# Inverse root of the head outputs: a power on GpSimd and a DRAM row in place of a product with a diagonal

## The chip, the cores and the metric

The program runs on one core of a Trainium2 chip. Its measure is the device time of one execution in microseconds (us), median over the runs. Below, PE is TensorE, DVE is VectorE, ACT is ScalarE, POOL is GpSimd and SP is SyncE; "PEld" is TensorE's weight load, and a "q" behind an engine's name is its instruction queue.

## The reference, cut to what matters

The model has two layers over 512 tokens of width 1024. Layer 0 is a differential attention with 8 heads, followed by a convolutional gated MLP and a gated embedding. Only the attention's last step, the norm of each head's output over its 128 columns, is touched:

```python
def rmsnorm(x, g):
    xf = x.astype(jnp.float32)
    inv = lax.rsqrt(jnp.mean(xf * xf, axis=-1, keepdims=True) + RMS_EPS)
    return (xf * inv).astype(x.dtype) * g

def diff_attention(...):
    ...
    o = lax.map(one_block, (q_blocks, jnp.arange(n_blocks)))
    o = o.transpose(1, 0, 3, 2, 4).reshape(B, S, N_HEADS, V_DIM)
    o = rmsnorm(o, sub_g) * (1.0 - lambda_init)
    return o.reshape(B, S, N_HEADS * V_DIM) @ w_o
```

All matrix products are made exact to float32 by splitting each operand into a high and a low part (three products of high and low for each one of the reference).

## The kernel before, in words

Weights come in 190 units of 512 KB into four raw slots (`w_raw`); SP issues a load as soon as DVE has made the low part of the unit that held the slot (`lo_done`). ACT makes the high part (`split_hi`, L383), DVE the low part (`split_lo`, L804), and PE uses them. The activations stand transposed: features on the 128 partitions, the 512 tokens along the free dimension.

The order of every engine is written out by hand in the program, one block for each engine, and semaphores join them. The attention runs in a loop over heads, `for hd in range(N_HEADS)`, that each engine has a copy of. For head hd, PE does:

- the key projection (24 products of 512 columns into bank 1), then half of the query projection into bank 0, the ten transposes of the weights of head hd-1 (`head_transposes`, L1347), the rest of the query projection;
- `output_spread(hd - 2)`: two products of 512 columns, a matrix of ones with a diagonal matrix, into bank 6 (L1263, L1264);
- `head_product(hd - 1)`: softmax weights by values, into bank 1 (L1238 to L1240 with wT and v);
- the scores of head hd (L1334), and `output_sums(hd - 1)`: sums of squares over the partitions, one column for each token tile (L1258).

DVE copies the keys out (`k_rows`, L902), then for head hd-2 makes the inverse of the root (`output_inverse`: L965, and the helper `spread` with L818, L820 and L822, which writes the diagonal `diag`), the low parts of keys, transposed weights (L954) and queries (L910), the norm of head hd-2 (`output_norm`, L971) with its low part (L976), then the maxima of the scores (`softmax_first`, L926, and L915, which ACT's exponentials wait for), the variance of head hd-1 (`output_variance`, L960) and the second half of the softmax (L936 to L943). ACT does the root of head hd-2 (`output_rms`, L477), the high parts of keys (L447), transposed weights (L456), queries (L451) and of the normed output (L462), the square (L466) and the scaled copy (L473) of head hd-1's output, and the exponentials (L485). The root and the exponential are in different tables, so that a table load stands ahead of each of the two in every head from 2 on.

So the norm of a head goes: variance, root on ACT, inverse and diagonal on DVE, product on PE (which turns the four columns of 128 tokens into a row of 512 that stands in all partitions), product with the output on DVE. It is done one head late. Heads 6 and 7 are normed behind the loop, beside the first products of the output projection (`wo_part`). The copy of a head's output, `o32`, is the buffer `acc`.

Of the kernel before, what the change touches and what calls it, by code (L numbers as in the profile page):

```python
# [8 lines left out]
F32 = mybir.dt.float32  # L9
F32R = mybir.dt.float32r  # L10
BF16 = mybir.dt.bfloat16
ALU = mybir.AluOpType
# [3 lines left out]
P = 128  # L16
# [19 lines left out]
GROUP = SEQ // P  # L36
N_GROUPS = N_HEADS // GROUP
FFN_PARTS = (8, 8, 6)
SLOTS = 4
# [55 lines left out]

def hybrid_trunk(nc, gain_and_x0, xT, pT, weights, final_gain, columns, out):
    with ExitStack() as ctx:
        def sem(name):
            return ctx.enter_context(nc.semaphore(name))

        def sb(name, shape, dt, scope=ctx):
            return scope.enter_context(nc.sbuf_tensor(name, shape, dt))
# [9 lines left out]
        oT_hi = sb("oT_hi", [P, N_HEADS, SEQ], F32R, product)  # L112
        oT_lo = sb("oT_lo", [P, N_HEADS, SEQ], F32R, product)
        product.close()
        product = ExitStack()
# [25 lines left out]
        eps = sb("eps", [P, 1], F32)  # L141
        small = sb("small", [P, 116], F32)
        bs = sb("bs", [P, KT], F32)
# [16 lines left out]
        v_lo = sb("v_lo", [P, TT, N_GROUPS, SEQ], F32R, attn)  # L160
        o32 = acc
        attn.close()
# [50 lines left out]
            sem("pv_done"), sem("o32_done"), sem("osq_done"), sem("oss_done"), sem("ovar_done"), sem("orms_done"),  # L213
            sem("oicol_done"), sem("odiag_done"), sem("ospread_done"))
        onorm_done, ohi_done, olo_done = sem("onorm_done"), sem("ohi_done"), sem("olo_done")

# [55 lines left out]
        orms_col = small[:, 4:8]  # L272
        oicol = small[:, 60:64]
        lam_product = small[:, 64:66]
        oeps = [small[:, 68:72], small[:, 72:76]]
# [5 lines left out]
        final_inv = small[:, 100:104]  # L281
        table_scratch = small[:, 80:81]


# [89 lines left out]
        def _(act):  # L374
# [83 lines left out]
            def output_high(hp):  # L458
                act.wait_ge(onorm_done, hp + 1)
                if hp == 0:  # L460
                    act.wait_ge(pT_done, DEPTH * PLE_KT)
                act.activation(oT_hi[:, hp, :], o32[:, :], ACT.Copy).then_inc(ohi_done, 1)  # L462

# [4 lines left out]
            def output_copy(hp, src):  # L468
                if hp == 0:
                    act.wait_ge(subg_done, 1)  # L470
                else:
                    act.wait_ge(olo_done, hp)
                act.activation(o32[:, :], src[:, :], ACT.Copy, scale=sub_g_scaled).then_inc(o32_done, 1)  # L473
# [283 lines left out]
        def _(pool):  # L757
# [10 lines left out]
                               pattern=[[-1, P]], channel_multiplier=1).then_inc(mask_done, 1)  # L768

            pool.wait_ge(evac_done, result_of("wo", KT - 1))  # L770
            for g, win in enumerate(POOL_WINDOWS):
# [25 lines left out]
        def _(dve):  # L797
# [159 lines left out]
            def output_variance(hp, src):  # L957
                dve.wait_ge(oss_done, hp + 1)
                dve.wait_ge(oeps_done, hp + 1)
                dve.scalar_tensor_tensor(out=ovar, in0=src[:, 0:TT], scalar=float(D_MODEL // P), in1=oeps[hp % 2],  # L960
                                         op0=ALU.mult, op1=ALU.add).then_inc(ovar_done, 1)

            def output_inverse(hp):
                dve.wait_ge(orms_done, hp + 1)
                dve.reciprocal(oicol, orms_col).then_inc(oicol_done, 1)  # L965
                dve.wait_ge(oicol_done, hp + 1)
                spread(oicol, oparts_done, 2 * hp).then_inc(odiag_done, 1)

            def output_norm(hp):
                dve.wait_ge(ospread_done, hp + 1)  # L970
                dve.scalar_tensor_tensor(out=o32[:, :], in0=bank[6][:, :], scalar=float(D_MODEL), in1=o32[:, :],  # L971
                                         op0=ALU.mult, op1=ALU.mult).then_inc(onorm_done, 1)

            def output_low(hp):
                dve.wait_ge(ohi_done, hp + 1)
                dve.tensor_tensor(oT_lo[:, hp, :], o32[:, :], oT_hi[:, hp, :].bitcast(F32), ALU.subtract).then_inc(olo_done, 1)  # L976

# [254 lines left out]
        def _(pe):  # L1232
# [89 lines left out]
            def scores(hd):  # L1322
# [43 lines left out]
            def output_spread(hp):  # L1366
                pe.wait_ge(odiag_done, hp + 1)
                spread(bank[6]).then_inc(ospread_done, 1)
# [30 lines left out]
            for hd in range(1, N_HEADS):  # L1399
# [329 lines left out]
```

## Time and profile before

| what | value |
|---|---|
| time, median of 3 runs | 1112.18 us (1111.61 to 1112.74) |
| span of the profiled execution, first to last instruction | 1110.7 us |
| mean granted TensorE clock, of full speed | 0.995 (1.00 in every stretch between 27 and 260 us) |
| busy: PE, DVE, ACT, POOL | 1093.1, 732.4, 537.4, 19.6 us |
| loop over heads 2 to 7 | about 83 to 188 us of the span |
| one head, from one group of transposes to the next | 17.56 us |
| in 142 to 160 us: PE, DVE, ACT busy | 18.00, 15.63, 14.61 us |

The page gives no time for the profiled execution but its span; the median of the runs is 1.5 us above it.

How to read it. In a timeline the columns are start (us from the span's start), duration (us), engine, source line, operation, output<-inputs, shapes, count; in square brackets stands how long the engine sat idle before, and who ended that. Products are pipelined: a product of 512 columns shows 0.39 us, yet the next starts 0.23 us later, so PE's time is read from starts, not from durations. A list of waits gives who waited for whom, the total in us, how often, and the longest. A group of the page or of the lines gives count | busy us, mean ns of one | idle before. An issue of a transfer gives KB each and the median us from issue to landing.

### The profile page before, as it was taken

The page shows a single profiled execution, that of the slowest core. Times are in us where ns is not written, and L with a number is a line of the kernel's source. Part 1 is how long each engine was busy: PE and PEld are TensorE (multiplying, and loading weights), DVE is VectorE, ACT ScalarE, POOL GpSimd, SP SyncE. Part 2 cuts the span into 40 slices and gives each one's busy share as a digit, 9 for nine tenths or more (in the row PEclk, how much of TensorE's full clock was granted, in tenths as well). Part 3 has the DMA queues.
Part 4 walks back from the last instruction along what each step waited for, and adds up shares of the span by engine and source line. Part 5 has one row for each costly group of instructions (what it writes and reads, how often), then busy time and mean ns, then how long its engine had stood idle before and what let it go on. Part 6 is the DMA issues. An engine that isn't in the chain of part 4 may idle for free.

```text
span 1110.7 us, 14486 instructions
## 1 busy us (share of the span) xinstructions
PE 1093.1 (98%) x5164; PEld 911.0 (82%) x5164; DVE 732.4 (66%) x1136; ACT 537.4 (48%) x799; POOL 19.6 (2%) x62
## 2 busy tenths in 40 slices
PE   9999999999999999999999999999999999999994
PEld 8878888888888888888888888888888888888884
DVE  6568888575775377744776878777437763476836
ACT  6458878454643144421445676544214442244645
POOL 0000000020000000000000000000000000000012
PEclk9999999999999999999999999999999999999997
DMA  8112121222233222332234222232322233222302
GB/s 325 64 58 74 42 76 57 73 101 110 83 107 114 76 95 94 98 116 84 97 98 133 95 76 76 88 102 94 114 76 94 95 103 118 75 101 95 136 36 76
DMA packets 30625, 106.31 MB, mean 96 GB/s; under 512 B 3312, under 2 KB 3312, under 8 KB 30576
## 3 DMA queue, kind: packets, MB, share of 16 engines
q1 hardware_dynamic: 30288, 105.13, 28.1%
q8 instruction: 30, 0.49, 0.2%
q10 hardware_dynamic: 288, 0.53, 0.1%
q14 instruction: 19, 0.16, 0.0%
HBM read 103.55 MB, written 2.10 MB: 95 GB/s over the span
## 4 chain that ended last, share of the span: by engine, by line
PE 92%; DVE 4%; ACT 3%; issue 1%; POOL 0%; DVEq 0%; ACTq 0%; POOLq 0%
PE bank L1238 29%; PE bank L1240 29%; PE bank L1239 29%; PE bank L1334 1%; PE bank L1258 1%; DVE h_tok L1183 1%; ACT probs L485 1%; DVE w_lo L804 1%; DVE c L1189 1%; PE bank L1347 1%; DVE c L1181 0%; PE bank L1299 0%; PE bank L1529 0%; PE bank L1613 0%; PE bank L1526 0%
## 5 line engine op out<-in xcount | busy, mean ns | idle before, releaser
L1238 PE MATMUL bank<-x_hi,w_hi 128*128 128x512 f32 x896 | 350.4, 391 | 0.0
L1240 PE MATMUL bank<-x_hi,w_lo 128*128 128x512 f32 x896 | 348.8, 389 | 0.0
L1239 PE MATMUL bank<-x_lo,w_hi 128*128 128x512 f32 x896 | 348.6, 389 | 0.0
L804 DVE TENSOR_TENSOR w_lo<-w_raw,w_hi 128x1024 fp32r<-128x1024 f32 (+1 forms) x189 | 226.0, 1197 | 52.7 <-ACT w_hi L383 52.6
L383 ACT ACTIVATE w_hi<-w_raw 128x1024 fp32r<-128x1024 f32 (+1 forms) x189 | 193.8, 1031 | 109.8 <-PE bank L1240 109.3
L1240 PEld LDWEIGHTS bank<-x_hi,w_lo 128*128 128x128 f32 x896 | 168.2, 188 | 35.3
L1238 PEld LDWEIGHTS bank<-x_hi,w_hi 128*128 128x128 f32 x896 | 168.2, 188 | 34.7 <-issue 0.4
L1239 PEld LDWEIGHTS bank<-x_lo,w_hi 128*128 128x128 f32 x896 | 168.2, 188 | 34.6
L1238 PE MATMUL bank<-g_hi,w_hi 128*128 128x512 f32 x352 | 136.9, 389 | 0.0
L1239 PE MATMUL bank<-g_lo,w_hi 128*128 128x512 f32 x352 | 136.9, 389 | 0.0
L1240 PE MATMUL bank<-g_hi,w_lo 128*128 128x512 f32 x352 | 136.9, 389 | 0.0
L630 ACT ACTIVATE c<-u,params 128x512 f32<-128x512 f32 x88 | 71.9, 817 | 107.2 <-DVE u L1106 107.2
L1106 DVE TENSOR_TENSOR u<-bank,inv 128x512 f32<-128x512 f32 x88 | 60.6, 689 | 92.6 <-PE bank L1240 92.5
L1012 DVE TENSOR_TENSOR gain_and_h<-bank,gain_and_h 128x512 f32<-128x512 f32 x56 | 38.5, 688 | 97.9 <-PE bank L1240 97.9
L637 ACT ACTIVATE g_hi<-g 128x512 f32 (+1 forms) x44 | 27.8, 632 | 118.8 <-DVE g L1122 118.8
L1239 PEld LDWEIGHTS bank<-g_lo,w_hi 128*128 128x128 f32 x352 | 66.1, 188 | 13.8
L1238 PEld LDWEIGHTS bank<-g_hi,w_hi 128*128 128x128 f32 x352 | 66.1, 188 | 13.7
L1240 PEld LDWEIGHTS bank<-g_hi,w_lo 128*128 128x128 f32 x352 | 66.1, 188 | 13.7
L1116 DVE SCALAR_TENSOR_TENSOR c<-u,params,c 128x512 f32<-128x512 f32 x88 | 66.2, 752 | 9.7 <-DVE c L1111 1.1
L1111 DVE SCALAR_TENSOR_TENSOR c<-u,params,c 128x512 f32<-128x512 f32 x88 | 66.0, 750 | 2.6 <-ACT c L630 1.2
L635 ACT ACTIVATE s<-c 128x512 f32<-128x512 f32 x44 | 27.8, 633 | 74.6 <-DVE c L1116 74.6
L1124 DVE TENSOR_TENSOR g_lo<-g,g_hi 128x512 f32 (+1 forms) x44 | 30.5, 693 | 38.2 <-ACT g_hi L637 38.2
(205 smaller groups left out, 1211.0 us busy)
## 6 DMA issues: line engine op xcount, KB each, us to landing
w_raw<-in_weights SPq DMA_DIRECT2D x189, 512.0 KB, 3.5
gain_and_h<-in_xT SPq DMA_DIRECT2D x7, 256.0 KB, 6.1
out<-emb SPq DMA_DIRECT2D x3, 512.0 KB, 3.1
p_raw<-in_pT SPq DMA_DIRECT2D x1, 1024.0 KB, 10.3
w_raw<-in_weights SPq DMA_DIRECT2D x2, 256.0 KB, 3.6
gain_b<-in_final_gain SPq DMA_DIRECT2D x1, 512.0 KB, 4.2
gain_and_h<-in_gain_and_x ACTq DMA_DIRECT2D x1, 260.0 KB, 3.4
params<-in_columns SPq DMA_DIRECT2D x1, 256.0 KB, 8.1
```

The source lines that it names most:

```text
L383: act.activation(w_hi[s][:, 0:w], w_raw[s][:, 0:w], ACT.Copy).then_inc(hi_done, 1)
L630: act.activation(c32[:, c, :], u32[:, c, PAD:PAD + SEQ], ACT.Identity, scale=tap(layer, 2, j + c * FT), bias=conv_bias(layer, j + c * FT)) ...
L635: act.activation(s32[:, :], c32[:, 0, :], ACT.Silu).then_inc(silu_done, 1)
L804: dve.tensor_tensor(w_lo[s][:, 0:w], w_raw[s][:, 0:w], w_hi[s][:, 0:w].bitcast(F32), ALU.subtract).then_inc(lo_done, 1)
L1012: dve.tensor_tensor(h[:, m, :], src, h[:, m, :], ALU.add).then_inc(evac_done, 1)
L1106: dve.tensor_tensor(u32[:, c, PAD:], bank[2 * v + c][:, :], inv[:, :], ALU.mult).then_inc(evac_done, 1)
L1111: dve.scalar_tensor_tensor(out=c32[:, c, :], in0=u32[:, c, PAD - 1:PAD - 1 + SEQ], scalar=tap(layer, 1, j + c * FT), in1=c32[:, c, :], op0 ...
L1116: dve.scalar_tensor_tensor(out=c32[:, c, :], in0=u32[:, c, PAD - 2:PAD - 2 + SEQ], scalar=tap(layer, 0, j + c * FT), in1=c32[:, c, :], op0 ...
L1124: dve.tensor_tensor(g_lo[:, 2 * a + v, :], g32[:, :], g_hi[:, 2 * a + v, :].bitcast(F32), ALU.subtract).then_inc(glo_done, 1)
L1238: pe.matmul(dst, w1, m1, start=start and i == 0, stop=False)
L1239: pe.matmul(dst, w1, m0, start=False, stop=False)
L1240: last = pe.matmul(dst, w0, m1, start=False, stop=stop and i == len(parts) - 1)
```

## The change

For heads 0 to 5 (`ROW_HEADS` is 6) the way from the variance to the row of inverse roots is another one. POOL raises the variance to the power -0.5 (one operation on 128 x 4 numbers for each head, `tensor_tensor` with `pow` and a constant `minus_half`). ACT, behind its exponentials, issues a transfer of these 512 numbers to a row in DRAM (`row_out`), and in the next head, behind the high part of the keys, waits for it to land and issues a second one that reads the row back into all 128 partitions (`row_in`, into `o_inv`). DVE multiplies by `o_inv` from SBUF in place of bank 6. `output_rms`, `output_inverse` and `output_spread` go for these heads; heads 6 and 7 keep them. The copy `o32` now alternates between two buffers (a new `o32_even` and `acc`), so that `output_copy` waits for the low part of the head before the previous one; and PE no longer waits for `onorm_done` ahead of the last score tile, since bank 6 is not written by a spread in the loop any more.

```diff
+            def row_out(hp):
+                act.wait_ge(opow_done, hp + 1)
+                act.dma_start(o_rows[hp].rearrange("(t p) -> p t", p=P), orow_col, allow_slow_non_contiguous=True).then_inc(orow_out, 16)
+
+            def row_in(hp):
+                act.wait_ge(orow_out, 16 * (hp + 1))
+                if hp:
+                    act.wait_ge(onorm_done, hp)
+                act.dma_start(o_inv[:, :], o_rows[hp:hp + 1, :].broadcast_to((P, SEQ))).then_inc(orow_in, 16)
...
             for hd in range(N_HEADS):
                 split_hi(FIRST_KQ + 2 * hd + 2)
+                k_high(hd)
                 if hd >= 2:
-                    output_rms(hd - 2)
-                k_high(hd)
+                    row_in(hd - 2)
...
                 exps(hd)
+                if 1 <= hd < last:
+                    row_out(hd - 1)
...
+            for hp in range(ROW_HEADS):
+                pool.wait_ge(ovar_done, hp + 1)
+                if hp:
+                    pool.wait_ge(orow_out, 16 * hp)
+                pool.tensor_tensor(orow_col, ovar, minus_half, ALU.pow).then_inc(opow_done, 1)
...
             def output_norm(hp):
+                o = o32[hp % 2][:, :]
+                dve.wait_ge(o32_done, hp + 1)
+                if hp < ROW_HEADS:
+                    dve.wait_ge(orow_in, 16 * (hp + 1))
+                    dve.tensor_tensor(o, o_inv[:, :], o, ALU.mult).then_inc(onorm_done, 1)
...
                 k_rows(hd)
-                if hd >= 2:
-                    output_inverse(hd - 2)
                 k_low(hd)
...
-                    if qt == TT - 1 and hd >= 2:
-                        pe.wait_ge(onorm_done, hd - 1)
...
-                if hd >= 2:
-                    output_spread(hd - 2)
                 pe.wait_ge(k32_done, hd + 1)
                 head_product(hd - 1, bank[1])
```

Three places show the new order; the names are those of the tiles. First ACT, from the weight split that opens a head to the exponentials (`probs`) of the same head; before:

```order
L383 ACTIVATE w_hi<-w_raw 128x1024
L477 ACT_TABLE_LOAD
L477 ACTIVATE small<-small 128x4
L447 ACTIVATE k_hi<-sq 128x512
L456 ACTIVATE wT_hi<-bank 128x512
L456 ACTIVATE wT_hi<-bank 128x384 x2
L451 ACTIVATE q_hi<-bank 128x512
L383 ACTIVATE w_hi<-w_raw 128x1024
L462 ACTIVATE oT_hi<-acc 128x512
L466 ACTIVATE sq<-bank 128x512
L473 ACTIVATE acc<-bank,small 128x512
L485 ACT_TABLE_LOAD
```

The same stretch now, with the transfer out ahead of it:

```order
L492 DMA o_rows<-small 128x4x1
L393 ACTIVATE w_hi<-w_raw 128x1024
L457 ACTIVATE k_hi<-sq 128x512
L499 DMA o_inv<-o_rows 128x512
L466 ACTIVATE wT_hi<-bank 128x512
L466 ACTIVATE wT_hi<-bank 128x384 x2
L461 ACTIVATE q_hi<-bank 128x512
L393 ACTIVATE w_hi<-w_raw 128x1024
L472 ACTIVATE oT_hi<-o_even 128x512
L476 ACTIVATE sq<-bank 128x512
L483 ACTIVATE acc<-bank,small 128x512
L507 ACTIVATE probs,small<-probs,small 128x128 x2
```

Two table loads and the root went from each head from 2 on (12 loads in all); two issues of transfers came, the second between the keys' and the transposed weights' high parts.

Second DVE, from the keys to the low part of the output (`oT_lo`); before:

```order
L902 TENSOR_TENSOR sq<-bank,inv 128x512
L965 RECIPROCAL small<-small 128x4
L818 CAST col_parts<-small 128x4
L820 TENSOR_TENSOR col_parts<-small,col_parts 128x4
L822 TENSOR_TENSOR diag<-ident,col_parts 128x1024
L906 TENSOR_TENSOR k_lo<-sq,k_hi 128x512
L954 TENSOR_TENSOR wT_lo<-bank,wT_hi 128x512
L954 TENSOR_TENSOR wT_lo<-bank,wT_hi 128x384 x2
L910 TENSOR_TENSOR q_lo<-bank,q_hi 128x512
L971 SCALAR_TENSOR_TENSOR acc<-bank,acc 128x512
L976 TENSOR_TENSOR oT_lo<-acc,oT_hi 128x512
```

and now:

```order
L934 TENSOR_TENSOR sq<-bank,inv 128x512
L938 TENSOR_TENSOR k_lo<-sq,k_hi 128x512
L986 TENSOR_TENSOR wT_lo<-bank,wT_hi 128x512
L986 TENSOR_TENSOR wT_lo<-bank,wT_hi 128x384 x2
L942 TENSOR_TENSOR q_lo<-bank,q_hi 128x512
L1009 TENSOR_TENSOR o_even<-o_inv,o_even 128x512
L1017 TENSOR_TENSOR oT_lo<-o_even,oT_hi 128x512
```

The four instructions of the inverse and the diagonal are gone; the norm reads `o_inv`, which a transfer fills.

On PE the only change in order is that the two products with `diag` between the query projection and the head product are gone for six heads (3567 rows before, 3555 now).

## Rows read from the trace of the kernel before

**Rows 1.** The page: the chain that ended last, by engine.

```profile
PE 92%; DVE 4%; ACT 3%; issue 1%; POOL 0%; DVEq 0%; ACTq 0%; POOLq 0%
```

**Rows 2.** List of waits, PE's own, 54 to 225 us.

```profile
PE bank L1238 <- DVE wT_lo L954: 0.9, 2, 0.5
```

**Rows 3.** Timeline, PE, head 4 and the start of head 5.

```profile
125.77 1.25 PE L1347 MATMUL bank<-ident,probs 128*128 128x128 f32 x10
...
129.63 0.39 PE L1263 MATMUL bank<-diag,ones_r 128*128 128x512 f32 x1
...
130.08 0.40 PE L1238 MATMUL bank<-wT_hi,v_hi 128*128 128x512 f32 x1
...
132.03 0.33 PE L1334 MATMUL bank<-k_hi,q_hi 64*128 64x128 f32 x2
...
134.14 1.05 PE L1258 MATMUL bank<-ones,sq 128*128 128x1 f32 x8
...
143.33 1.25 PE L1347 MATMUL bank<-ident,probs 128*128 128x128 f32 x10
```

**Rows 4.** Timeline, ACT, the same stretch.

```profile
132.32 0.58 ACT L466 ACTIVATE sq<-bank 128x512 f32<-128x512 f32 x1
...
133.88 1.28 ACT L485 ACT_TABLE_LOAD   x1
...
139.50 0.80 ACT L485 ACTIVATE probs<-probs,small 128x512 f32<-128x512 f32 x1
...
144.01 0.63 ACT L447 ACTIVATE k_hi<-sq 128x512 fp32r<-128x512 f32 x1 [1.15 <-DVE sq L902]
```

**Rows 5.** Timeline, DVE, the same stretch.

```profile
130.46 0.69 DVE L910 TENSOR_TENSOR q_lo<-bank,q_hi 128x512 fp32r<-128x512 f32 x1 [0.17 <-ACT q_hi L451]
...
134.28 0.16 DVE L915 TENSOR_TENSOR small<-small 128x4 f32<-128x4 f32 x1
...
136.73 0.16 DVE L960 SCALAR_TENSOR_TENSOR small<-bank,small 128x4 f32<-128x4 f32 x1
...
140.42 0.17 DVE L936 RECIPROCAL small<-small 128x2 f32<-128x2 f32 x1 [0.64 <-ACT probs L485]
...
143.29 0.69 DVE L902 TENSOR_TENSOR sq<-bank,inv 128x512 f32<-128x512 f32 x1
```

**Rows 6.** Timeline, all engines, head 7 before its head product.

```profile
180.63 1.34 ACT L456 ACTIVATE wT_hi<-bank 128x512 fp32r<-128x512 f32 x3
...
181.37 1.22 DVE L804 TENSOR_TENSOR w_lo<-w_raw,w_hi 128x1024 fp32r<-128x1024 f32 x1
...
182.51 1.15 DVE L954 TENSOR_TENSOR wT_lo<-bank,wT_hi 128x512 fp32r<-128x512 f32 x2
...
182.56 0.40 PE L1264 MATMUL bank<-diag,ones_r 128*128 128x512 f32 x1
...
183.34 0.47 PE L1238 MATMUL bank<-wT_hi,v_hi 128*128 128x512 f32 x1 [0.39 <-DVE wT_lo L954]
```

**Rows 7.** Timeline, POOL beside DVE at the kernel's end.

```profile
1080.89 1.68 POOL L792 TENSOR_TENSOR emb<-h_tok,gain_b 128x512 f32<-128x512 f32 x1 [0.63 <-DVE h_tok L1183]
...
1081.45 1.67 DVE L1183 TENSOR_TENSOR h_tok<-c,h_tok 128x512 f32<-128x512 f32 x1
...
1087.52 0.69 DVE L1183 TENSOR_TENSOR h_tok<-c,h_tok 128x512 f32<-128x512 f32 x1
```

**Rows 8.** Groups of lines, POOL: its smallest operation that reads SBUF.

```profile
L785 POOL TENSOR_SCALAR_AFFINE_SELECT edge<-edge 128x16 f32<-128x16 f32 x4 | 1.6, 442 | 0.0
```

**Rows 9.** The page: issues of transfers (median us from issue to landing).

```profile
w_raw<-in_weights SPq DMA_DIRECT2D x189, 512.0 KB, 3.5
...
p_raw<-in_pT SPq DMA_DIRECT2D x1, 1024.0 KB, 10.3
...
out<-emb ACTq DMA_DIRECT2D x1, 256.0 KB, 3.0
```

**Rows 10.** Timeline, ACT's queue, its first issue.

```profile
0.82 0.41 ACTq L393 DMA_DIRECT2D gain_and_h<-in_gain_and_x  x1
```

More of the change, by code:

```diff
@@ L37 @@
 N_GROUPS = N_HEADS // GROUP
+ROW_HEADS = N_HEADS - 2
 FFN_PARTS = (8, 8, 6)
@@ L93, in result_of, with hybrid_trunk @@
     return RESULTS_BEFORE[name] + u + 1
-def hybrid_trunk(nc, gain_and_x0, xT, pT, weights, final_gain, columns, out):
+def hybrid_trunk(nc, gain_and_x0, xT, pT, weights, final_gain, columns, out, o_rows):
     with ExitStack() as ctx:
@@ L113, in hybrid_trunk @@
         oT_lo = sb("oT_lo", [P, N_HEADS, SEQ], F32R, product)
+        product.close()
+        product = ExitStack()
+        before_last_head = sb("before_last_head", [P, N_HEADS - 1, SEQ], F32, product)
+        o_inv = sb("o_inv", [P, SEQ], F32, product)
+        before_last_low = sb("before_last_low", [P, N_HEADS - 1, SEQ], F32, product)
+        o32_even = sb("o32_even", [P, SEQ], F32, product)
         product.close()
@@ L141, in hybrid_trunk @@
         eps = sb("eps", [P, 1], F32)
-        small = sb("small", [P, 116], F32)
+        small = sb("small", [P, 120], F32)
         bs = sb("bs", [P, KT], F32)
@@ L160, in hybrid_trunk @@
         v_lo = sb("v_lo", [P, TT, N_GROUPS, SEQ], F32R, attn)
-        o32 = acc
+        o32 = [o32_even, acc]
         attn.close()
@@ L273, in hybrid_trunk @@
         oicol = small[:, 60:64]
+        orow_col = small[:, 116:120]
         lam_product = small[:, 64:66]
@@ L282, in hybrid_trunk @@
         table_scratch = small[:, 80:81]
+        minus_half = small[:, 0:4]
         NORM_MIX0, NORM_FFN0, NORM_PLE0, NORM_MIX1, NORM_FFN1, NORM_PLE1 = range(6)
@@ L461, in output_high @@
                     act.wait_ge(pT_done, DEPTH * PLE_KT)
-                act.activation(oT_hi[:, hp, :], o32[:, :], ACT.Copy).then_inc(ohi_done, 1)
+                act.activation(oT_hi[:, hp, :], o32[hp % 2][:, :], ACT.Copy).then_inc(ohi_done, 1)
             def output_square(hp, src):
@@ L470, in output_copy @@
                     act.wait_ge(subg_done, 1)
-                else:
-                    act.wait_ge(olo_done, hp)
-                act.activation(o32[:, :], src[:, :], ACT.Copy, scale=sub_g_scaled).then_inc(o32_done, 1)
+                if hp >= 2:
+                    act.wait_ge(olo_done, hp - 1)
+                act.activation(o32[hp % 2][:, :], src[:, :], ACT.Copy, scale=sub_g_scaled).then_inc(o32_done, 1)
             def output_rms(hp):
@@ L959, in output_variance @@
                 dve.wait_ge(oeps_done, hp + 1)
+                if hp:
+                    dve.wait_ge(opow_done, min(hp, ROW_HEADS))
                 dve.scalar_tensor_tensor(out=ovar, in0=src[:, 0:TT], scalar=float(D_MODEL // P), in1=oeps[hp % 2],
@@ L963, in output_inverse @@
             def output_inverse(hp):
-                dve.wait_ge(orms_done, hp + 1)
+                nth = hp - ROW_HEADS
+                dve.wait_ge(orms_done, nth + 1)
                 dve.reciprocal(oicol, orms_col).then_inc(oicol_done, 1)
-                dve.wait_ge(oicol_done, hp + 1)
-                spread(oicol, oparts_done, 2 * hp).then_inc(odiag_done, 1)
+                dve.wait_ge(oicol_done, nth + 1)
+                spread(oicol, oparts_done, 2 * nth).then_inc(odiag_done, 1)
             def output_norm(hp):
-                dve.wait_ge(ospread_done, hp + 1)
-                dve.scalar_tensor_tensor(out=o32[:, :], in0=bank[6][:, :], scalar=float(D_MODEL), in1=o32[:, :],
-                                         op0=ALU.mult, op1=ALU.mult).then_inc(onorm_done, 1)
+                o = o32[hp % 2][:, :]
[3 more added lines that the diff above has]
+                    dve.tensor_tensor(o, o_inv[:, :], o, ALU.mult).then_inc(onorm_done, 1)
+                else:
+                    dve.wait_ge(ospread_done, hp - ROW_HEADS + 1)
+                    dve.scalar_tensor_tensor(out=o, in0=bank[6][:, :], scalar=float(D_MODEL), in1=o,
+                                             op0=ALU.mult, op1=ALU.mult).then_inc(onorm_done, 1)
             def output_low(hp):
                 dve.wait_ge(ohi_done, hp + 1)
-                dve.tensor_tensor(oT_lo[:, hp, :], o32[:, :], oT_hi[:, hp, :].bitcast(F32), ALU.subtract).then_inc(olo_done, 1)
+                dve.tensor_tensor(oT_lo[:, hp, :], o32[hp % 2][:, :], oT_hi[:, hp, :].bitcast(F32), ALU.subtract).then_inc(olo_done, 1)
             last = N_HEADS - 1
@@ L1366, in output_spread @@
             def output_spread(hp):
-                pe.wait_ge(odiag_done, hp + 1)
+                pe.wait_ge(odiag_done, hp - ROW_HEADS + 1)
                 spread(bank[6]).then_inc(ospread_done, 1)
@@ L1725 @@
     result = nc.dram_tensor("out", (1, SEQ, D_MODEL), F32, kind="ExternalOutput").ap()
-    hybrid_trunk(nc, *args, result)
+    o_rows = nc.dram_tensor("o_rows", (ROW_HEADS, SEQ), F32, kind="Internal").ap()
+    hybrid_trunk(nc, *args, result, o_rows)
     r = run_bass_kernel_spmd(nc, [arrays], core_ids=[0])
```

3 lines of the change are left out of this document (added).

## The prediction

> **What bounds the kernel now.** I read the chain that ended last first: PE holds 92% of it [rows 1]. Then PE's own waits over the attention: 0.9 us in two waits, both for the low part of the transposed weights [rows 2]; one of the two is head 7's, 0.39 us [rows 6], the other is head 1's, which the change doesn't touch. Then one head from transposes to transposes: 143.33 - 125.77 = 17.56 us with PE never idle [rows 3]. So heads 2 to 6 cost what PE issues in them, and PE's issues are read from starts: the first product with the diagonal starts at 129.63, the head product at 130.08, so the two products cost 0.45 us, not the 0.78 that their durations add up to.
>
> ACT and DVE matter only by their slack to PE: ACT's exponentials, DVE's softmax, keys and transposed weights [rows 4, 5].
>
> **What goes on PE.** Two products in each of six heads. In heads 2 to 6 they are on the path: 5 x 0.45 = 2.25 us. In head 7 the head product starts at 183.34, while the spread's second product started at 182.56 [rows 6] and so its first near 182.33: there 1.01 us lie between the end of the queries and the head product, most of it a wait for DVE. DVE is late because the four instructions of the inverse and the diagonal stood before the keys' low part, the weight split and the transposed weights. They go, but DVE's weight split then waits for ACT's, which ends when ACT's transposed weights start, at 180.63, and in the new order stands behind one more issue of 0.41 us [rows 6, 10]: 181.04 in place of 181.37. The head product comes 0.33 us earlier. Together 2.25 + 0.33 = 2.58 us.
>
> **What goes on DVE and ACT.** Four DVE instructions in each head; DVE was not the bound, so by themselves nothing. On ACT a table load of 1.28 us before the exponentials [rows 4], one before the root, and the root. The load before the exponentials ended at 135.16, while the first maxima were negated at 134.28 + 0.16 = 134.44 [rows 5]: the first exponentials can start 0.7 us earlier, the later ones wait for the second group of maxima (done just before 136.73) and gain about 0.5. The rest of the softmax, the weight split and the keys on DVE come 0.5 us earlier with them, which matches the 0.45 by which PE comes earlier. So in the new head DVE and ACT stand to PE as before, and nothing is gained beyond PE's own 0.45.
>
> **What is late next.** The scores wait for the queries' low part: that ends at 130.46 + 0.69 = 131.15, the scores start at 132.03 [rows 3, 5], 131.58 after the change: 0.4 us of slack left. The queries' parts hang on PE's projection and not on what was removed, so this slack stays.
>
> **The new way of the row, against its deadlines.** Times are those of rows 3 to 5 with the shifts above. The variance is ready at 136.73 + 0.16 = 136.89. POOL's power stands in no row. Its nearest row is POOL's 128 x 16 selection with 0.44 us; the longest arithmetic operation of POOL in this trace is 1.68 us [rows 7, 8]. For 128 x 4 numbers I take 0.5, with 0.2 and 1.7 as ends. ACT comes to the transfer out behind the exponentials: the last one started at 139.50 and lasts 0.80 [rows 4], 0.5 earlier gives 139.8. So a power of up to 2.9 us is not waited for there.
>
> The row must have landed when ACT has made the keys' high part: 144.01 - 0.5 + 0.55 = 144.05. That is 4.25 us from the issue. If it is later, ACT holds up the transposed weights. The way from there to PE is 0.41 for the issue [rows 10], about 0.6 for the first high part, and 183.34 - 182.51 = 0.83 from the start of DVE's low part to the product [rows 6]: 145.9, against a head product that PE reaches at 129.63 + 17.56 - 0.45 = 146.74. Slack 0.85 us.
>
> The second transfer leaves ACT near 144.05. DVE wants the row behind the queries' low part, at 131.15 + 17.56 - 0.45 = 148.25. If it is later, the normed output's high part on ACT is late, and with it the square that PE's sums wait for. The square ends at 132.90, the sums come at 134.14 - 0.45 = 133.69 [rows 3, 4]: slack 0.8 us. So the second transfer has 4.2 us without any effect and 5.0 without an effect on PE; both together have 149.05 - 139.8 = 9.2 us.
>
> What a transfer takes: 3.0 us for 256 KB from ACT, 3.5 for the 512 KB of a weight unit, 10.3 for 1 MB in the crowd at the start [rows 9]. The second one (128 pieces of 2 KB) is of the first kind; I take 3.3. The first is 512 pieces of 4 bytes and no row shows such a one: 3.0 is the low end, the 10.3 of `p_raw`, which is cut into 512 pieces too, the high end. I take 4.0, near the small ones, since `p_raw` had 1 MB to move behind other loads. A weight unit is loaded at the same moment (DVE's split frees its slot), which is why I don't take 3.0. The sum is 7.3 of 9.2 us, and 4.0 of the 4.25 + 0.85 for the first alone: hidden. With 10.3 it isn't.
>
> The Trainium skill (DMA: Bandwidth & Descriptors, "Rules for kernel authors") says that an access whose last dimension is strided becomes one descriptor for each element and should be rearranged, and its "Specifications" say that below 512 B the engines read, modify and write. It gives no time for either, no run here shows one yet, and the sum doesn't use it. It speaks against the 4.0 and for the first rival.
>
> The second buffer for `o32` saves ACT a wait and PE nothing. The wait of the last scores for the norm was never waited for [rows 2]: nothing.
>
> **Sum.** 1110.7 - 2.6 = 1108.1 us of span. The median stands 1.5 us above the span of the profiled execution: 1112.18 - 2.6 = 1109.6 us.
>
> **Rivals.**
>
> First, the row is late. With a transfer of small pieces of, say, 5.6 us in place of 4.0, ACT stands 0.5 us beyond its slack in each head, and 6 x 0.5 = 3.0 us take back the 2.6: 1112.6. At 5.35 us half is taken back: 1111. For it speaks that the pieces are the smallest of the kernel and go out beside a weight load; against it that the landing times of rows 9 hardly depend on the size, so that they are mostly fixed cost. Its middle is 1111.5.
>
> Second, on the other side, the power holds up DVE. At the kernel's end POOL runs products of two SBUF operands, and DVE's product of two SBUF operands that starts in the middle of one lasts 1.67 us, where the same one alone lasts 0.69 [rows 7]: 1081.45 + 1.67 = 1083.12 is 0.55 behind the end of POOL's at 1082.57. DVE waited for POOL to end. The power starts right behind the variance, and DVE's next operation with two SBUF operands comes 0.2 us later. DVE's idle time before the second reciprocal, 0.64 us [rows 5], and the 0.85 us of slack of the transposed weights cover it: nothing happens up to a power of 0.15 + 0.64 + 0.85 = 1.65 us (in head 7 up to 0.8). Beyond it each us is one on PE in each head, and from 1.65 + 0.45 = 2.1 us the change loses. A power of 3.0 us costs 6 x 1.35 = 8.1, less 2.6: 1117.7; one of 2.5 us costs 5.1, less 2.6: 1114.7. For it speaks that a power is more than the selection or product of the rows; against it that there are four numbers in a partition where the 1.68 us stand for 512.
>
> The Trainium skill (SBUF — State Buffer, "Who interferes with whom") states this as an exclusive lock: a DVE instruction with two SBUF inputs blocks against a GpSimd instruction that reads SBUF, for the whole of it. By that rule the trace agrees (1.67 against 0.69 us); it is this rival, and where DVE would share the port instead, the rival would be gone.
>
> Third, the change does less than it says: something else that I take for slack, head 7's wait or the scores' 0.4 us, becomes the bound and eats a part. Only head 7's 0.33 gone and 0.2 us in each of the five heads give 2.6 - 1.3 = 1.3: 1110.9.
>
> **How the numbers follow.** A difference of 0.2% (2.2 us) is about what a measurement of this kernel can tell from none. Forecast 0.60 (1109.6, its own range 1109.0 to 1110.3; one time in six of it is within 0.2%); late row 0.20 (mostly within 0.2%, a quarter of it slower); DVE held up 0.12 (slower); does less 0.08 (within). Faster 0.51, same 0.32, slower 0.17. The range reaches down to 1108.8 (head 7 gives its whole 1.01 us and the rest falls out a little better) and up to 1114.0, which takes in the late row and a power of up to 2.4 us, and leaves out its longer ones and the 10.3 us transfer.
>
> **What would show it.** Right: one head takes 17.1 us on PE; no wait of PE in heads 2 to 6; ACT's first exponential right behind the first negated maxima; the head product of head 7 less than 0.8 us behind the queries; transfers out and in landing within 5.1 and 5.0 us of their issue; a power below 1.65 us. Wrong: PE waits for `wT_lo` (row out late, or DVE held up, told apart by ACT's idle time before `row_in` and by a stretched DVE operation beside POOL's) or for the square (row in late); a head of more than 17.56 us.

## The result and the profile after

| | before | after |
|---|---|---|
| device time, median | 1112.46 us (1111.61 to 1112.81, 4 runs) | 1151.39 us (1151.30 to 1151.64, 4 runs) |
| span of the profiled execution | 1110.7 us | 1149.9 us |
| head 4, transposes to transposes | 17.56 us | 23.89 us |

The ratio is 1.0353, 95% interval 1.0338 to 1.0368: the kernel is 3.5% slower. The prediction said 1109.6 us, at most 1114.0.

The chain that ended last, by engine and by line (the page of the kernel after):

```profile
PE 84%; DMA 6%; DVE 6%; ACT 3%; issue 1%; ACTq 0%; POOL 0%; DVEq 0%; POOLq 0%
PE bank L1277 27%; PE bank L1279 27%; PE bank L1278 27%; DMA o_rows<-small 6%; DVE probs L958 2%; PE bank L1371 1%; ACT probs L507 1%; DVE h_tok L1222 1%; DVE c L1228 1%; PE bank L1297 1%; DVE w_lo L836 1%; DVE c L1220 0%; DVE wT_lo L986 0%; PE bank L1338 0%; ACT w_hi L393 0%
```

A DMA stands on the chain that had none [rows 1]: `o_rows<-small`, the transfer out with the 512 inverse roots. The list of waits from 54 to 260 us gives the way from it to PE (us in total, times, longest):

```profile
DVE wT_lo L986 <- ACT wT_hi L466: 32.4, 6, 6.9
ACT wT_hi L466 <- DMA o_rows<-small: 31.8, 5, 6.9
PE bank L1277 <- DVE wT_lo L986: 29.5, 7, 5.8
...
ACT w_hi L393 <- DMA o_rows<-small: 5.8, 1, 5.8
...
DVE o_even L1009 <- DMA o_inv<-o_rows: 2.8, 3, 1.2
```

PE's 0.9 us [rows 2] became 29.5: head 1's 0.49 (0.51 before) and six waits of 4.3 to 5.75 us, one before the head product of each of heads 2 to 7. Behind each stands ACT, which must issue the transfer in. For that it waits until the transfer out has landed, and the high part of the transposed weights stands behind this issue in its program (in head 7 the weight split, the `w_hi` line). The issues of the same stretch (median us from issue to landing last):

```profile
w_raw<-in_weights SPq DMA_DIRECT2D x20, 512.0 KB, 10.2
o_inv<-o_rows ACTq DMA_DIRECT2D x6, 256.0 KB, 4.4
o_rows<-small ACTq DMA_DIRECT2D x6, 2.0 KB, 12.0
```

2 KB take 12.0 us (11.5 to 12.6 over the six). And the weight units, 3.5 us over the whole kernel before [rows 9], take 10.2 in this stretch. No engine waits for a weight unit here. That the small transfer is what makes them late is shown by experiments 4 and 7. ACT's timeline in head 4 (start, duration, engine and line, in brackets the idle time before and what ended it):

```profile
134.18 0.38 ACTq L492 DMA_DIRECT2D o_rows<-small  x1
...
139.70 0.63 ACT L457 ACTIVATE k_hi<-sq 128x512 fp32r<-128x512 f32 x1 [2.67 <-DVE sq L934]
...
145.96 0.33 ACTq L499 DMA_DIRECT2D o_inv<-o_rows  x1
146.33 1.36 ACT L466 ACTIVATE wT_hi<-bank 128x512 fp32r<-128x512 f32 x3 [6.00 <-DMA o_rows<-small]
```

ACT starts the keys' high part at 139.70. In experiment 1 below, where the row is in time, the issue of the transfer in comes 0.06 us behind that start; here it comes at 145.96, 6.2 us late. PE in the same head, to the transposes of the next:

```profile
139.48 1.25 PE L1384 MATMUL bank<-ident,probs 128*128 128x128 f32 x10
...
143.11 0.39 PE L1279 MATMUL bank<-x_hi,w_lo 128*128 128x512 f32 x1
147.80 0.76 PE L1277 MATMUL bank<-wT_hi,v_hi 128*128 128x512 f32 x1 [4.30 <-DVE wT_lo L986]
148.36 0.63 PE L1278 MATMUL bank<-wT_lo,v_hi 128*128 128x512 f32 x1
148.79 0.63 PE L1279 MATMUL bank<-wT_hi,v_lo 128*128 128x512 f32 x1
...
163.37 1.25 PE L1384 MATMUL bank<-ident,probs 128*128 128x128 f32 x10
```

After the wait the products lie 0.43 us apart, before it 0.23. The table of stretches shows why (us, busy time of PE, PEld, DVE, ACT, POOL, granted clock, DMA's share, GB/s):

```profile
139.00:147.00 8.00, 4.50 (x25) 3.48 (x23) 1.39 (x4) 1.30 (x3) 0.00 (x0) 0.93 0.63 56
147.00:151.00 4.00, 3.20 (x11) 2.94 (x11) 2.75 (x5) 2.13 (x4) 0.00 (x0) 0.50 0.56 184
151.00:163.00 12.00, 12.00 (x71) 10.12 (x70) 9.73 (x33) 7.99 (x20) 1.01 (x1) 0.93 0.49 7
```

After 4.3 us of idling PE is granted 0.50 from 147 to 151 us, the 1.2 GHz level. So each late row is paid twice. Head 4, from 139.48 to 163.37, took 23.89 us with a wait of 4.30 in it. Without a late row a head takes 17.13 (experiment 1 below), so 23.89 - 17.13 - 4.30 = 2.46 us are the clock's.

The same sum can be made for every head. The transposes start at 90.42, 115.40, 139.48, 163.37, 187.44, 211.40 and 236.01 us, and the waits in heads 2 to 7 are 5.25, 4.50, 4.30, 4.64, 4.60 and 5.75 us, 29.0 together. Head 7 takes 17.37 us without a wait (17.60 less 0.23 in experiment 2). What is left over in the six heads is 2.60, 2.45, 2.46, 2.30, 2.23 and 1.49, together 13.5 us for the slower clock (0.86 granted on average in each of them). Experiment 2 takes 2.8 us less than before over these heads, and 0.2 of its time is still a wait; 29.0 + 13.5 - 2.8 - 0.2 = 39.5 us. The profiled executions differ by 39.2 (1149.9 - 1110.7), the medians by 38.9.

### The profile page after: what moved, and what is told of

The parts are those of the page before. It is cut to its first block, busy times and chain, and to the rows that moved or that the text cites. A ratio compares the mean times of both kernels' runs of the same rounds, so it can differ in the third digit from the quotient of the medians.

```text
span 1149.9 us, 14458 instructions
## 1 busy us (share of the span) xinstructions
PE 1103.8 (96%) x5152; PEld 919.5 (80%) x5152; DVE 723.9 (63%) x1112; ACT 521.9 (45%) x781; POOL 25.7 (2%) x69
## 4 chain that ended last, share of the span: by engine, by line
PE 84%; DMA 6%; DVE 6%; ACT 3%; issue 1%; ACTq 0%; POOL 0%; DVEq 0%; POOLq 0%
PE bank L1277 27%; PE bank L1279 27%; PE bank L1278 27%; DMA o_rows<-small 6%; DVE probs L958 2%; PE bank L1371 1%; ACT probs L507 1%; DVE h_tok L1222 1%; DVE c L1228 1%; PE bank L1297 1%; DVE w_lo L836 1%; DVE c L1220 0%; DVE wT_lo L986 0%; PE bank L1338 0%; ACT w_hi L393 0%
## 5 line engine op out<-in xcount | busy, mean ns | idle before, releaser
L1155 DVE SCALAR_TENSOR_TENSOR c<-u,params,c 128x512 f32<-128x512 f32 x88 | 66.2, 752 | 10.3 <-DVE c L1150 2.1
```

The costliest lines, as they stand in the source:

```text
L1155: dve.scalar_tensor_tensor(out=c32[:, c, :], in0=u32[:, c, PAD - 2:PAD - 2 + SEQ], scalar=tap(layer, 0, j + c * FT), in1=c32[:, c, :], op0 ...
```

## The experiments

Each is measured against the kernel before on the same chip. In the short diffs the minus lines are those of the change, line numbers are left out and `...` stands for arguments or lines left out; `row_out` and `row_in` are the change's two functions on ACT.

**1. Only the order of the row in DRAM.** Each partition writes its four numbers side by side, 128 pieces of 16 bytes in place of 512 of 4; the norm reads the row with a stride.

```diff
-act.dma_start(o_rows[hp].rearrange("(t p) -> p t", p=P), orow_col, ...)
+act.dma_start(o_rows[hp].rearrange("(p t) -> p t", t=TT), orow_col)
-dve.tensor_tensor(o, o_inv[:, :], o, ALU.mult)
+dve.tensor_tensor(o.rearrange("q (t p) -> q t p", p=P),
+    o_inv[:, :].rearrange("q (p t) -> q t p", t=TT), o.rearrange("q (t p) -> q t p", p=P), ALU.mult)
```

> The change with one difference: the transfer out writes each partition's four numbers as one piece of 16 bytes (128 pieces in place of 512 of 4 bytes), and the norm reads the row with a stride of 16 bytes. Theory A (the transfer out is late because of its 512 single numbers, about 9.5 us over a fixed 2.5, so in proportion to the pieces): it lands 4 to 5 us after its issue, PE's waits in heads 2 to 6 are gone or under 0.5 us each, time 1109 to 1112. Theory B (a small write to DRAM waits for the weight load beside it, whatever its pieces): it lands after about 12 us as before, time near 1151. The strided read may add up to 0.7 us to the norm on DVE, which the slack of 0.8 us hides.

Measured: 1109.22 us (8 runs) against 1112.02 (15 runs), ratio 0.9974 (0.9963 to 0.9984). Same waits, same order on every engine, same bytes, and the loss is gone. The issues from 54 to 240 us:

```profile
w_raw<-in_weights SPq DMA_DIRECT2D x24, 512.0 KB, 3.5
o_inv<-o_rows ACTq DMA_DIRECT2D x6, 256.0 KB, 3.7
o_rows<-small ACTq DMA_DIRECT2D x6, 2.0 KB, 1.4
```

PE, transposes to transposes: 125.05 - 107.92 = 17.13 us.

```profile
107.92 1.25 PE L1385 MATMUL bank<-ident,probs 128*128 128x128 f32 x10
125.05 1.25 PE L1385 MATMUL bank<-ident,probs 128*128 128x128 f32 x10
```

The strided norm takes 1.07 us in place of 0.69 and is hidden. This version computes the reference and is faster than both kernels (0.26% faster than the one before).

**2. No transfer out at all.** The transfer in reads a constant row of the same size; heads 0 to 5 are normed by that constant.

```diff
-act.wait_ge(orow_out, 16 * (hp + 1))
-act.dma_start(o_inv[:, :], o_rows[hp:hp + 1, :].broadcast_to((P, SEQ)))
+act.dma_start(o_inv[:, :], final_gain[0:1, 0:SEQ].broadcast_to((P, SEQ)))
-if 1 <= hd < last:
-    row_out(hd - 1)
```

> The power stays, the transfer out is left out, and the transfer in reads a constant row of the final gain and waits for nothing (the norm of heads 0 to 5 is wrong). This is the change without its late part. The prediction's sum gives 1109.9 (2.6 us below 1112.46): 17.1 us for a head and no wait of PE in heads 2 to 6, head product of head 7 0.3 us earlier. Rival: the power on POOL (1.0 us) holds up DVE and eats part of it: 1110.5 to 1112.

Measured: 1109.12 us (7 runs) against 1112.02, ratio 0.9973 (0.9962 to 0.9984), 2.9 us less; a head takes 17.13 us. PE's waits for the transposed weights, 54 to 240 us (head 1's 0.51 and head 7's 0.23):

```profile
PE bank L1272 <- DVE wT_lo L981: 0.7, 2, 0.5
```

So the gain on PE is what the prediction summed up, and a transfer out of 1.4 us (experiment 1) is as good as none.

**3. The power alone.** The power on GpSimd stays, but the numbers are spread by the products with a diagonal as before, for heads 0 to 5; both transfers go.

```diff
-dve.wait_ge(orow_in, 16 * (hp + 1))
-dve.tensor_tensor(o, o_inv[:, :], o, ALU.mult)
+dve.wait_ge(opow_done, hp + 1)
+spread(orow_col, oparts_done, 2 * hp)
+...
+dve.scalar_tensor_tensor(out=o, in0=bank[6][:, :], scalar=float(D_MODEL), in1=o,
+                         op0=ALU.mult, op1=ALU.mult)
```

> One part alone: POOL's power in place of the root and the reciprocal for heads 0 to 5, with the diagonal and its product on PE kept and no transfers. ACT loses 12 table loads and the root. If PE alone sets the pace of the loop, nothing is gained on it: 17.56 us for a head; only head 7's wait may shrink by 0.2 us (one DVE instruction fewer before the weight split): 1111.8 to 1112.2 with before at 1112.0, same. Rival (ACT's relief is worth something by itself): 1110 or less. Rival (POOL's power blocks DVE): DVE's operation behind the variance stretched from 0.22 to over 1 us, slower.

Measured: 1111.59 us (10 runs) against 1112.07 (19 runs), ratio 0.9995 (0.9986 to 1.0005): no difference. A head takes 17.57 us, as before. PE's wait in head 7 is gone (one wait of 0.5 us is left). POOL beside DVE's next operation in this kernel's timeline:

```profile
102.99 1.01 POOL L796 TENSOR_TENSOR small<-small 128x4 f32<-128x4 f32 x1 [16.47 <-DVE small L990]
103.01 0.22 DVE L966 SCALAR_TENSOR_TENSOR small<-small 128x2 f32<-128x2 f32 x1
```

DVE starts 0.02 us behind the power, and its 0.22 us are what the same operation takes at 106.16, where POOL is idle. The next two operations on DVE (`probs`, two operands in SBUF) take 0.75 us together, both begun inside the power. In head 7, where no power runs, the three take 0.22 and 0.75 us as well. So the power of 1.01 us holds up none of them.

**4. Nobody waits for the transfer out.** It is issued as in the change, but the transfer in reads the constant row (heads 0 to 5 are normed by it) and does not wait.

```diff
-act.wait_ge(orow_out, 16 * (hp + 1))
-act.dma_start(o_inv[:, :], o_rows[hp:hp + 1, :].broadcast_to((P, SEQ)))
+act.dma_start(o_inv[:, :], final_gain[0:1, 0:SEQ].broadcast_to((P, SEQ)))
```

> The transfer out stays as in the change, but the transfer in reads a constant row of the final gain instead and no longer waits for it (so heads 0 to 5 are normed with wrong numbers). Theory A (what costs is ACT's wait for the landing, with PE's slower clock behind it): the transfer out still lands after about 12 us, nobody on the path waits, time near 1110. Theory B (what costs is that the small writes hold up the weight loads, whose landing went from 3.5 to 10 us): time stays well above 1112, with waits of ACT's weight split for loads.

Measured: 1140.64 us (4 runs) against 1112.02, ratio 1.0250 (1.0235 to 1.0266). The wait was taken away and most of the loss stayed. The issues from 54 to 240 us, then the waits:

```profile
w_raw<-in_weights SPq DMA_DIRECT2D x18, 512.0 KB, 9.2
o_inv<-in_final_gain ACTq DMA_DIRECT2D x6, 256.0 KB, 9.6
o_rows<-small ACTq DMA_DIRECT2D x6, 2.0 KB, 11.1
```

```profile
PE bank L1296 <- ACT sq L476: 17.8, 6, 4.3
...
DVE acc L1008 <- DMA o_inv<-in_final_gain: 11.6, 3, 5.0
DVE o_even L1008 <- DMA o_inv<-in_final_gain: 10.6, 3, 4.2
```

The transfer in took 3.7 us in experiments 1 and 2. It takes 9.6 here, though nothing in the program makes it wait; what is new beside it is the transfer out. PE now waits for the square, which ACT makes behind the norm. The account closes here too: heads 2 to 7 take 134.4 us (103.2 in experiment 2), 31.2 more, of which 17.8 are the six waits; the other 13.4 go with a granted clock of 0.85 to 0.92 in these heads.

**5. The same, with the transfer in done once.** As experiment 4, but the constant row comes in for head 0 alone.

```diff
-if hp:
-    act.wait_ge(onorm_done, hp)
+if hp:
+    return
-dve.wait_ge(orow_in, 16 * (hp + 1))
+dve.wait_ge(orow_in, 16)
```

> The transfer out stays as in the change (512 adjacent pieces of 4 bytes), nobody waits for it, and the transfer in is issued only once, for head 0, from a constant (the norm of heads 0 to 5 is wrong). It splits what the run in which nobody waits still lost (28 us): if that was the late transfer in (9.6 us in place of 3.7), it is gone and the time is 1109 to 1111, though weight loads still land after 9 to 10 us. If the late weight loads cost by themselves, ACT's weight splits wait for them and the time stays above 1115.

Measured: 1117.6 us (1114.94 to 1118.9, 4 runs) against 1112.24 (7 runs), ratio 1.0046 (1.0028 to 1.0064). The issues, then PE's waits:

```profile
w_raw<-in_weights SPq DMA_DIRECT2D x23, 512.0 KB, 10.0
o_inv<-in_final_gain ACTq DMA_DIRECT2D x1, 256.0 KB, 10.3
o_rows<-small ACTq DMA_DIRECT2D x6, 2.0 KB, 12.4
```

```profile
PE bank L1296 <- ACT sq L476: 4.5, 1, 4.5
PE bank L1276 <- DVE wT_lo L985: 0.7, 2, 0.5
```

One transfer in, of 10.3 us, gives one wait of 4.5. From there on a head takes 17.13 us although each still has a transfer out of 12 us and weight units of 10 beside it. By its time alone the run falls on the side of the late weights (above 1115), but no engine waits for a weight load in this stretch. So the late weights cost PE nothing, and what costs is a transfer that somebody needs before it lands, here within about 5 us. The profiled execution is 7.5 us longer than that of experiment 2 (1114.9 against 1107.4), and head 2 alone makes up 7.2 of them: it takes 24.37 us, which is 17.13, the wait of 4.47, and 2.77 with a clock of 0.50 behind it. The medians are 8.5 apart; the executions spread over 4 us here, and the last 1 us isn't explained.

**6. Six shapes of the transfer out.** One in each head, nobody waits for them, the transfer in reads the constant row (heads 0 to 5 are normed by it); three are repeated at the kernel's end by SP, when no weights are loaded any more.

```diff
-act.dma_start(o_rows[hp].rearrange("(t p) -> p t", p=P), orow_col, ...)
+hp == 0: o_rows[hp].rearrange("(t p) -> p t", p=P)    # the change's shape
+hp == 1: o_rows[hp].rearrange("(p t) -> p t", t=TT)   # 128 x 16 bytes, adjacent
+hp == 2: o_rows[hp, 0:P], orow_col[:, 0:1]            # 128 x 4 bytes, adjacent
+hp == 3: into SBUF, 8 bytes apart in each partition   # 512 x 4 bytes
+hp == 4: o_wide[:, :, 0:1]                            # 512 x 4 bytes, 512 bytes apart
+hp == 5: o_rows[hp, 0:2 * P], orow_col[:, 0:2]        # 256 x 4 bytes, adjacent
```

> As the run in which nobody waits (the row in is a constant, so the norm is wrong), but each head sends its four columns out in another form: head 0 512 pieces of 4 bytes to a DRAM row, head 1 128 of 16 bytes, head 2 128 of 4 bytes (one column), head 3 512 of 4 bytes to SBUF, head 4 512 of 4 bytes to DRAM 512 bytes apart, head 5 256 of 4 bytes; and three of them again on SP's queue near the end, when no weights are loaded. Number of pieces as the cause: landings of about 12, 5, 5, 12, 12, 7.5 us, the quiet ones the same. Writes to DRAM below 512 bytes as the cause: the one to SBUF lands in about 3.5 us. Neighbouring pieces in one line as the cause: the one 512 bytes apart lands clearly earlier than 12 us. Contention with the weight load as the cause: the quiet ones land in 3 to 4 us and the others all near 12.

Measured, us from issue to landing (one execution, 1126.89 us): 11.1, 3.1, 8.3, 2.2, 2.4, 8.4. At the end of the kernel, with DMA otherwise quiet:

```profile
L370 SPq DMA_DIRECT2D o_rows<-small x1: 377/377/377, 1074.4 to 1074.4; - x1
DMA to landing us min/median/max: 9.7/9.7/9.7
```

The same there for 16 bytes 1.4, for 512 bytes apart 2.1. The 3.1 of head 1 (128 pieces of 16 bytes) isn't explained; experiment 1's six take 1.4 to 2.8. Two fall as main causes: the number of pieces (512 take 2.1 to 2.4 us where they lie apart or go to SBUF, and 256 side by side take no longer than 128) and the weight load beside it (9.7 us without one). What is left is small pieces side by side in DRAM.

**7. That form in every head.** 512 pieces of 4 bytes, 512 bytes apart in DRAM; nobody waits, the transfer in reads the constant row (heads 0 to 5 are normed by it).

```diff
-act.dma_start(o_rows[hp].rearrange("(t p) -> p t", p=P), orow_col, ...)
+act.dma_start(o_wide[:, :, 0:1], orow_col.rearrange("p (t o) -> p t o", o=1), ...)
```

> As the run in which nobody waits (the row in is a constant, the norm of heads 0 to 5 is wrong), but all six transfers out write their 512 pieces of 4 bytes 512 bytes apart in DRAM. Theory C (neighbouring 4-byte pieces within the same stretch of DRAM hold each other up, and the stalled DMA engines hold up all other transfers): landing near 2.4 us, weight loads back at 3.5 us, time 1109.2 as without the transfer. Theory A (the number of pieces): time near 1140 as in the run where nobody waits.

Measured: 1109.15 us (10 runs) against 1112.07, ratio 0.9976 (0.9966 to 0.9985). The issues from 54 to 240 us:

```profile
w_raw<-in_weights SPq DMA_DIRECT2D x24, 512.0 KB, 3.5
o_inv<-in_final_gain ACTq DMA_DIRECT2D x6, 256.0 KB, 3.7
o_wide<-small ACTq DMA_DIRECT2D x6, 2.0 KB, 2.1
```

Against experiment 4 only the addresses differ: the count of DMA packets on ACT's queue is the same (4032 in this stretch). The 31.5 us between the two (1140.64 - 1109.15), the late weights and the late transfer in are gone with the close addresses.

**8 to 10. How close is too close.** As experiment 6, with six shapes each into an unused DRAM array; heads 0 to 5 are normed by the constant row.

```diff
-act.dma_start(o_rows[hp].rearrange("(t p) -> p t", p=P), orow_col, ...)
+act.dma_start(o_flat[...].rearrange("(p s) -> p s", s=STEP)[:, 0:N], orow_col[:, 0:N], ...)
```

> The row in is a constant again. Head by head 128 pieces go out with another distance in DRAM: 4 bytes every 64, 32, 16 and 8 bytes, then 8 bytes adjacent, then 4 bytes adjacent. Theory C with a line of 64 bytes: the first lands in 2 to 3 us, those with 2 and 4 pieces in a line rise only if the pieces of a line come from different DMA engines, those with 8 and 16 approach the 8.3 us that the adjacent ones took. Theory D (it is adjacency alone, contiguous addresses): all spaced ones land in 2 to 3 us and the two adjacent ones in about 8.

> The row in is a constant again. 128 pieces in each head: 16 bytes adjacent and aligned to 64; the same shifted by 32 bytes; 4 bytes every 16, shifted by 32; 16 bytes every 128, shifted by 56 (each crosses a 64-byte line that no other piece touches); 16 bytes adjacent, shifted by 16; 4 bytes adjacent. Theory C (pieces that different DMA engines write into one 64-byte line hold each other up; an engine serves four partitions in a row, so 16-byte steps keep a line with one engine only where they are aligned): aligned 1.4 us, the three shifted adjacent ones about 4 us as with 8-byte steps, the crossing one 1.4 to 2. Theory D (a piece or step of 16 bytes is enough whoever writes it): all of 16 bytes 1.4 us, shifted or not.

> The six transfers out are replaced by six shapes to an unused DRAM array; the transfer in reads a constant and waits for none of them, so the output norm is not the reference's. So far, from issue to landing: pieces 16 bytes apart or more 1.4 us wherever they begin, 4 bytes every 8 bytes 4.1, 8 bytes adjacent 4.4, 4 bytes adjacent 8.0 to 8.7 (each 128 pieces), and 512 pieces of 4 bytes adjacent 11 to 12 us. Theory G: what costs is that several pieces of one transfer share an aligned block of 16 bytes. It expects for (head 0) 128 pieces of 4 bytes every 12 bytes: about 3 us, since one block in three is shared; (head 1) 512 adjacent pieces of 4 bytes where the four of a block come from one partition: 11 us or more; (head 2) 32 adjacent pieces of 4 bytes: between 1.4 and 8; (head 3) 128 pieces of 16 bytes, adjacent, shifted by 8 bytes, so that every block is shared by two: about 4 us; (head 4) 8 adjacent pieces: under 4; (head 5) the change's own shape: 11 to 12. Theory S: what costs is a piece of under 16 bytes with a neighbour closer than 16 bytes, wherever the blocks lie: head 3 1.4 us, the rest as above. Theory E: only pieces that different DMA engines write into one block hold each other up, and neighbours of one partition go out on one engine: head 1 2.0 to 2.5 us, head 3 about 4 us.

Measured, us from issue to landing (one execution of each kernel, so each shape stands here once; those of experiment 10 are read from the completion signals of the DMA engines, the last of which gives, for the shapes of experiment 8, the landing of its rows):

| pieces | us |
|---|---|
| 128 x 4 bytes every 64, 32, 16 bytes (8) | 1.4, 1.4, 1.4 |
| 128 x 4 bytes every 12 bytes (10) | 1.8 |
| 128 x 4 bytes every 8 bytes (8) | 4.1 |
| 128 x 8 bytes, adjacent (8) | 4.4 |
| 128 x 4 bytes, adjacent (8, 9) | 8.0, 8.7 |
| 32 and 8 x 4 bytes, adjacent (10) | 5.2, 1.2 |
| 128 x 16 bytes, adjacent; shifted by 32; by 16 bytes (9) | 1.4, 1.4, 1.7 |
| 128 x 4 bytes every 16 bytes, shifted by 32; 128 x 16 bytes every 128 bytes, shifted by 56 (9) | 1.4, 1.4 |
| 128 x 16 bytes, adjacent, shifted by 8 bytes (10) | 2.8 |
| 512 x 4 bytes, adjacent, the four of 16 bytes from one partition (10) | 7.2 |
| 512 x 4 bytes, the change's shape (10) | 9.4 |

The rows of the slowest and the fastest shape of experiment 8 (4 bytes adjacent, 4 bytes every 64):

```profile
L503 ACTq DMA_DIRECT2D o_flat<-small x1: 332/332/332, 172.0 to 172.0; - x1
DMA to landing us min/median/max: 8.0/8.0/8.0
...
L493 ACTq DMA_DIRECT2D o_flat<-small x1: 337/337/337, 85.2 to 85.2; - x1
DMA to landing us min/median/max: 1.4/1.4/1.4
```

The boundary lies between steps of 16 and 8 bytes. Where a line of 64 bytes begins has no effect (shifts by 32 and 56 bytes, counted from the start of the array). An aligned piece of 16 bytes takes 1.4 us and the same one shifted by 8, which shares two blocks of 16 with its neighbours, takes 2.8. So it isn't the size of the piece alone: the slow transfers of the last table are those whose pieces share an aligned block of 16 bytes (theory G). That is what the table suggests, not a law that it shows. Eight adjacent pieces share blocks too and take 1.2 us, and steps of 12 bytes take 1.8 against 1.7 for an aligned shape without sharing. The sizes that theory G named held in part: 1.8 where it said about 3, 2.8 for 4, 7.2 for at least 11, and 9.4 for the change's own shape, for which it said 11 to 12 (why it took 9.4 here, 11.1 in experiments 4 and 6 and 12.0 in the change stays open). That only pieces from different partitions hold each other up is out in its sharp form (7.2 where it said 2.0 to 2.5), though that form is quicker than the change's 9.4. What happens in the DMA engines or the memory when several pieces fall into one block isn't shown by these records.

## Why the prediction was wrong

**The step that failed** is the transfer out, "I take 4.0", with 5.1 us allowed. It took 12.0, and 1.4 with nothing but the order of the row changed (experiment 1). The trace of before had no transfer of small pieces, and I took the value near the transfers of large pieces because landing times hardly depended on size there. That argument was about size; what decides here is how the pieces lie in DRAM, which no row of before varied. The high end that I had written down, 10.3 us [rows 9], was near the truth (by another mechanism), and I left it out of the range with no row against it. By the prediction's own deadline it gives 10.3 - 5.1 = 5.2 us in each of six heads, 31.2 us less 2.6: 1140.8. The range should have reached there, and even that is 10.6 us short of 1151.39, since it has no term for the clock (13.5 us).

The Trainium skill (DMA: Bandwidth & Descriptors, "Rules for kernel authors") advised against just this access and I left it without weight for want of a number. The runs put numbers to it: 12.0 us as the change writes it, 1.4 once rearranged. They also show that one element in each descriptor is not by itself what costs, since 512 of them 512 bytes apart land in 2.1 us (experiment 7). Its "Specifications" name reading, modifying and writing below 512 B; all the shapes above are below 512 B and they spread from 1.2 to 12 us.

**The sum on PE was right in size.** 2.6 us predicted; with the transfer out away or fast 2.9, 2.8, 2.9 (experiments 2, 1, 7). A head was to take 17.11 us and took 17.13. Head 7 was mis-sized a little: its head product was to come 0.33 us earlier, and it comes 4.26 us behind the transposes in experiment 2 (180.00 - 175.74) and 4.64 in experiment 1 (181.07 - 176.43), against 4.87 before (183.34 - 178.47), so 0.61 and 0.23 earlier. A wait for the transposed weights stays in front of it in both, 0.23 and 0.62 us, where 0.39 stood [rows 6].

**Nothing gained on DVE and ACT by themselves: right.** Experiment 3 has the table loads and the root gone, and the time is that of before.

**Deadlines.** ACT issued the transfer out earlier than I had it: in experiment 1 at 120.59, which is 12.67 us behind the transposes at 107.92, where I had 139.8 - 125.77 = 14.03, since in the trace the issue stands ahead of the last two exponentials and not behind them. The row was wanted 126.15 - 120.59 = 5.6 us later, not 4.25. With the slack of 0.85 that leaves 12.0 - 6.4 = 5.6 us late; PE's waits were 4.3 to 5.75.

**The power.** 0.5 us taken, 1.01 measured, within the ends and below the 1.65 that were allowed (above head 7's 0.8): no effect, since DVE wasn't held up at all.

**The transfer in.** 3.3 us taken, 3.7 measured, hidden (4.4 in the change, where DVE waits for it, 1.4 us at most, and PE doesn't). It has 5.0 us; experiment 4's 9.6 show what lies beyond.

**Rivals.** The first, the late row, is what happened, with the wait at the place that it named (PE for `wT_lo`, ACT idle before `row_in`). Its price was wrong: I sized it for a landing of 5.6 us, and I counted only the wait, not PE's fall to the 1.2 GHz level behind it (1.5 to 2.6 us a head). That other transfers land late beside this one (experiment 4) I hadn't thought of; in the change itself it cost PE nothing. The second, the power holding up DVE, did not happen: 0.22 us beside the power and alone (experiment 3). Nor did the third, that the change does less than it says: 2.8 to 2.9 us came once the row was in time.

The Trainium skill (SBUF — State Buffer, "Who interferes with whom") has DVE's instruction with two SBUF inputs blocked for the whole of GpSimd's. [rows 7] agree with it at 512 numbers in a partition. The pair of experiment 3 doesn't, at 4 numbers in a partition: DVE's 0.22 us lie inside POOL's 1.01, and by the rule it would have ended after it. Since POOL's times in the profile are rough, how long the power reads SBUF isn't shown, and the pair doesn't refute the rule.

## What to carry to other kernels

A row written to DRAM from a column over partitions should be laid out so that each partition's numbers stand side by side in aligned pieces of 16 bytes (larger ones weren't tried), and the stride goes on the side of the engine that reads it (0.38 us here, against 10.6 us of landing). Where the profile has no row for a new form of transfer, the high end belongs into the range, and the wait behind it is to be priced with the clock that PE loses after idling (13.5 us beside 29.0 of waits here). A DMA that nobody waits for can still be the cause: compare the landing times of the others with those before it came.

## What the runs showed of the hardware

- Writes of 4 bytes side by side in DRAM: 12.0 us from issue to landing for 512 of them (change), 8.0 to 8.7 for 128 (experiments 6, 8, 9). 128 of them at steps of 16, 32 or 64 bytes: 1.4 (experiment 8). 512 of them 512 bytes apart 2.1 (experiment 7), into SBUF 2.2 (experiment 6).
- While such writes are under way, other transfers are late too: weight units land after 9.2 to 10.2 us in place of 3.5, a 256 KB row after 9.6 to 10.3 in place of 3.7 (the weight units in the change and experiments 4 and 5, the row in experiments 4 and 5). The landings that nobody needed soon cost nothing.
- A wait of PE of 4.30 us was followed by a granted clock of 0.50, and the head took 2.46 us more than its work and the wait.
- GpSimd's power of 128 x 4 numbers takes 1.01 us and did not hold up DVE (experiment 3).
- DVE's product of 128 x 512 numbers takes 1.07 us where one operand is read at a step of 16 bytes, 0.69 side by side (experiment 1).
